# RWKV-7 and S5 trunk on one core: token scale moved behind the FFN's first products, and token norms cut to 64 columns

## Reference, cut to what matters

```
def rmsnorm(x, g):
    y = xf * lax.rsqrt(jnp.mean(xf * xf, axis=-1, keepdims=True) + NORM_EPS)
    return (y * g)
# rwkv7: keys' norm
kk = kk / jnp.maximum(jnp.linalg.norm(kk, axis=-1, keepdims=True), 1e-12)
# layer
h = h + mix
hn = rmsnorm(h, norm_ffn[i])
ffn = (silu(hn @ w_gate) * (hn @ w_up)) @ w_down      # D=1024, F=2816
h = h + ffn
```

## Time and profile before

| | |
|---|---|
| median of three executions | 1642.6 us |
| the profiled execution | 1643.39 us |
| its span, first to last instruction | 1641.5 us |
| TensorE busy, VectorE busy, ScalarE busy | 1576.6 (96%), 1270.2 (77%), 958.2 (58%) us |
| mean granted TensorE clock | 0.979 of full speed |

### The profile page before, as it was taken

The page is one execution under the profiler, slowest core; times in us unless marked ns, Lnnn a source line. Parts: engine busy times, 40 slices in busy tenths (PEclk is TensorE's granted clock), DMA queues, the critical chain, the costliest instruction groups (busy, mean ns, idle before and its releaser), DMA issues.

```text
span 1641.5 us, 28526 instructions
## 1 busy us (share of the span) xinstructions
PE 1576.6 (96%) x12396; PEld 1359.9 (83%) x12396; DVE 1270.2 (77%) x1430; ACT 958.2 (58%) x1054; POOL 87.8 (5%) x71
## 2 busy tenths in 40 slices
PE   8898798899998999999999999999999999999997
PEld 7698787899998788788888888888888888888885
DVE  6675432996865546998988888888888898988985
ACT  2723211666441036776776776776776777777673
POOL 0006101100001600000000000000000000000000
PEclk9999999999996999999999999999999999999999
DMA  7230002444525064799799799799799799799791
GB/s 287 94 130 28 4 3 104 153 182 164 184 90 207 20 265 187 290 384 372 295 392 384 284 392 399 272 389 401 268 392 402 269 390 401 276 384 401 276 382 68
DMA packets 72493, 421.19 MB, mean 257 GB/s; under 512 B 5024, under 2 KB 5152, under 8 KB 37424
## 3 DMA queue, kind: packets, MB, share of 16 engines
q1 hardware_dynamic: 72016, 418.26, 65.5%
q0 software_dynamic: 352, 1.10, 0.2%
HBM read 418.29 MB, written 1.05 MB: 255 GB/s over the span
## 4 chain that ended last, share of the span: by engine, by line
PE 91%; DVE 4%; POOL 2%; issue 1%; ACT 1%; DVEq 0%; POOLq 0%
PE PS L1285 37%; PE PS L1298 18%; PE PS L1100 11%; PE PS L1208 3%; PE PS L1314 2%; PE PS L733 2%; PE PS L1085 2%; PE PS L710 2%; PE PS L1291 1%; PE PS L887 1%; PE PS L754 1%; PE PS L692 1%; PE PS L904 1%; DVE LOA L1791 1%; PE PS L1174 1%
## 5 line engine op out<-in xcount | busy, mean ns | idle before, releaser
L1791 DVE TENSOR_TENSOR LOA<-EXA,WH 128x2048 fp32r<-128x2048 f32 x224 | 504.7, 2289 | 94.1 <-ACT WH L598 94.1
L598 ACT ACTIVATE WH<-EXA 128x2048 fp32r<-128x2048 f32 x224 | 416.9, 1909 | 6.4 <-DMA EXA<-in_wmoe 6.2
L1285 PE MATMUL PS<-WH,XGH 128*128 128x512 f32 x896 | 360.6, 403 | 0.0
L1285 PE MATMUL PS<-WH,XGL 128*128 128x512 f32 x896 | 350.6, 391 | 0.0
L1285 PE MATMUL PS<-LOA,XGH 128*128 128x512 f32 x896 | 350.0, 391 | 0.0
L1797 DVE TENSOR_TENSOR LOB<-EXB,WH 128x1024 fp32r<-128x1024 f32 x224 | 264.3, 1222 | 8.6 <-ACT WH L602 8.5
L602 ACT ACTIVATE WH<-EXB 128x1024 fp32r<-128x1024 f32 x224 | 224.2, 1052 | 0.0
L1285 PEld LDWEIGHTS PS<-WH,XGL 128*128 128x128 f32 x896 | 168.2, 188 | 35.7
L1285 PEld LDWEIGHTS PS<-WH,XGH 128*128 128x128 f32 x896 | 168.4, 188 | 33.4 <-DVE XGL L1889 1.8
L1285 PEld LDWEIGHTS PS<-LOA,XGH 128*128 128x128 f32 x896 | 168.8, 188 | 31.2
L1298 PE MATMUL PS<-WH,MHH 128*128 128x512 f32 x448 | 174.6, 390 | 3.8 <-DVE MHL L1885 3.8
(11 more groups left out here) (413 smaller groups left out, 2410.9 us busy)
## 6 DMA issues: line engine op xcount, KB each, us to landing
EXA<-in_wmoe SPq DMA_DIRECT2D x112, 2048.0 KB, 8.6
EXB<-in_wmoe SPq DMA_DIRECT2D x112, 1024.0 KB, 8.1
FRA<-in_wffn SPq DMA_DIRECT2D x22, 1024.0 KB, 5.9
RING<-in_wsq SPq DMA_DIRECT2D x16, 1024.0 KB, 4.9
FRB<-in_wffn SPq DMA_DIRECT2D x22, 512.0 KB, 3.8
GLUW<-in_wglu SPq DMA_DIRECT2D x8, 1024.0 KB, 12.5
...
```

The source lines that it names most:

```text
L598: act.activation(WH[:, n % 4, 0:NARROW], EXA[PAIR_SLOT[n // 2]][:, n % 2, :], ACT.Copy).then_inc(S("m_ahi"), 1)
L1285: mm = pe.matmul(PS[:, p % 2, :], x[:, k, :], w, start=k == 0 and m == 0, stop=k == KC - 1 and m == 2)
L1791: tt(LOA[slot][:, n % 2, :], EXA[slot][:, n % 2, :], WH[:, n % 4, 0:NARROW].bitcast(F32), ALU.subtract)\
```

## The change

- Norm 1: FH and FL are now taken from `HT * gain` without the token scale, pair by pair while the output projection runs. The scale is multiplied onto both halves of gate and up's sums in one VectorE instruction per block (`FGU`, 128x512, out of PSUM), ahead of Silu, which now reads SBUF and waits for that instruction. VectorE multiplies the halves afterwards. Norm 1's last sums stand between gate and up of block 0. FFN slots are swapped so that block 0's weights can be loaded after item 12 and cut into high and low during items 14.
- Norms 0, 2, 4: the sums go to four strips of 32 partitions with 64 tokens each, NT has 64 columns, and a new `spread_rows` brings four strips back to 128 partitions in four banks, from which the products read.
- `spread` of the keys' norm stands behind split projection 2.
- FFN adds: four instructions, one per bank, each as soon as its bank's last matmul is done; squares in four.
- Item 12: halves in turn within each chunk. Item 13 writes bank 5 instead of 0.

```diff
+        SUM_BANK = (7, 7, 3, 0, 4)
+        SPREAD_BANK = {0: 3, 2: 4, 4: 0}
+        VARIED, SUMMED = (1, 3, 4, 6, 7), (1, 3, 4, 6, 7)
+        QT = T // 4
+        def spread_scale(n, chunks):
+            first = SPREAD_BANK[n]
+            return PS[:, first:first + 4, 0:QT].unsqueeze(1).to_broadcast([P, chunks, 4, QT])
@@ SyncE
                 if t < 2:
-                    sp.wait_ge(S("used"), 15)
+                    sp.wait_ge(S("used"), 13 + t)
...
                 sp.dma_start(FRA[:, t % 2, :], wffn[t][:, 0:NARROW]).then_inc(S(f"fa_in{t % 2}"), 16)
-                if t >= 2:
+                if t < 2:
+                    sp.wait_ge(S("used"), 15)
+                else:
                     sp.wait_ge(S("f_blo"), t - 1)
@@ ScalarE, output projection
             for t in range(4):
                 act.wait_ge(S("h_out"), t + 1)
+                for j in (2 * t, 2 * t + 1):
+                    act.activation(FH[:, j, :], HT[:, j, :], ACT.Copy, scale=prm("ffn0", j)).then_inc(S("f_hi"), 1)
                 square(1, SQB, slice(2 * t, 2 * t + 2))
+                if t == 1:
+                    ffn_hi_a(0, 0)
+                    ffn_hi_a(0, 1)
             act.wait_ge(S("used"), 16)
-            ffn_hi_a(0, 0)
+            ffn_hi_a(1, 0)
             root(1)
-            ffn_hi_a(0, 1)
-            ffn_hi_a(1, 0)
-            for n in range(4):
-                pair = slice(2 * n, 2 * n + 2)
-                act.wait_ge(S("n_out"), 8 + 2 * (n + 1))
-                act.activation(flat(FH[:, pair, :]), flat(HNF[:, pair, :]), ACT.Copy).then_inc(S("f_hi"), 1)
             ffn_hi_a(1, 1)
             ffn_hi_b(0)
@@ ScalarE, FFN
             for t in range(NFFN):
-                act.wait_ge(S("f_ps"), t + 1)
-                act.activation(FSG[:, t % 2, :], half(t % 3, 0), ACT.Silu).then_inc(S("f_silu"), 1)
+                act.wait_ge(S("f_mul"), 2 * t + 1)
+                act.activation(FGU[:, t % 2, 0, :], FGU[:, t % 2, 0, :], ACT.Silu).then_inc(S("f_silu"), 1)
                 round_back(t, 0)
                 if t + 2 < NFFN:
                     ffn_hi_a(t + 2, 0)
-                act.wait_ge(S("f_mul"), t + 1)
-                act.activation(FHH[:, t % 2, :], FHF[:, t % 2, :], ACT.Copy).then_inc(S("f_hh"), 1)
+                act.wait_ge(S("f_mul"), 2 * t + 2)
+                act.activation(FHH[:, t % 2, :], FGU[:, t % 2, 1, :], ACT.Copy).then_inc(S("f_hh"), 1)
...
-            for n, h in enumerate(halves):
-                act.wait_ge(S("h_out"), 5 + n)
-                square(2, SQB, h)
+            for g in range(NG):
+                act.wait_ge(S("h_out"), 5 + g)
+                square(2, SQ2, slice(2 * g, 2 * g + 2))
@@ TensorE
+                        for q in range(4):
+                            mm = pe.matmul(PS[32 * q:32 * q + 32, SUM_BANK[n], 0:QT], one[:, 0:32], sq[:, k, q * QT:(q + 1) * QT],
+                                           start=start and k == 0, stop=stop and k == KC - 1, skip_group_check=True)
...
+            def spread_rows(n):
+                pe.wait_ge(S("n_var"), VARIED[n] + 1)
+                for q in range(4):
+                    rows = slice(32 * q, 32 * q + 32)
+                    row = ROW0[rows, :] if n == 0 else CON[rows, C_SPR:C_SPR + P]
+                    mm = pe.matmul(PS[:, SPREAD_BANK[n] + q, 0:QT], row, NT[rows, 0:QT], start=True, stop=True)
+                mm.then_inc(S("n_sum"), 1)
...
             project_split(1, XRH, XRL)
+            project_split(2, XRH, XRL)
             pe.wait_ge(S("sig"), 16)
             pe.wait_ge(S("kk"), 3)
             for j in BY_QUARTER:
                 mm = spread(j, 4 + j // 2)
             mm.then_inc(S("kk_ps"), 1)
-            project_split(2, XRH, XRL)
             project_split(3, XRH, XRL)
...
+                steps = [(h, k) for k in range(KC) for h in range(2)] if t == 12 else [(h, k) for h in range(2) for k in range(KC)]
...
-            norm_part(1, SQB, 3, False, True, 2)
...
                 for h in range(2):
                     if t == 0 and h == 1:
+                        norm_part(1, SQB, 3, False, True, 2)
                         pe.wait_ge(S("f_alo"), 2)
...
+                    if t == NFFN - 1 and n in (1, 3, 5):
+                        mm.then_inc(S("f_ps"), 1)
...
             ffn_down(NFFN - 1)
-            pe.wait_ge(S("h_out"), 6)
-            norm(2, SQB)
+            for g in range(NG):
+                norm_part(2, SQ2, g, g == 0, g == NG - 1, 2)
+            spread_rows(2)
@@ VectorE
+            def scale_of_tokens(n):
+                dve.wait_ge(S("n_sum"), SUMMED[n])
+                ts(NT[:, 0:QT], PS[:, SUM_BANK[n], 0:QT], 1.0 / D, NORM_EPS, ALU.mult, ALU.add).then_inc(S("n_var"), 1)
                 dve.wait_ge(S("n_std"), n + 1)
+                dve.reciprocal(NT[:, 0:QT], NT[:, 0:QT]).then_inc(S("n_var"), 1)
+                dve.wait_ge(S("n_sum"), SUMMED[n] + 1)
...
             for t in range(4):
                 dve.wait_ge(S("used"), 12 + t + 1)
                 tt(flat(HT[:, 2 * t:2 * t + 2, :]), flat(HT[:, 2 * t:2 * t + 2, :]), PS[:, W_BANK[t], :], ALU.add).then_inc(S("h_out"), 1)
+                if t == 2:
+                    ffn_lo_a(0, 0)
+                    ffn_lo_a(0, 1)
+                dve.wait_ge(S("h_out"), t + 1)
+                for j in (2 * t, 2 * t + 1):
+                    dve.wait_ge(S("f_hi"), j + 1)
+                    stt(FL[:, j, :], HT[:, j, :], prm("ffn0", j), FH[:, j, :].bitcast(F32), ALU.mult, ALU.subtract).then_inc(S("f_lo"), 1)
+            dve.wait_ge(S("n_sum"), SUMMED[1])
+            ts(NT[:, :], half(SUM_BANK[1], 0), 1.0 / D, NORM_EPS, ALU.mult, ALU.add).then_inc(S("n_var"), 1)
             ffn_lo_a(1, 0)
+            dve.wait_ge(S("n_std"), 2)
+            link(dve.reciprocal(NT[:, :], NT[:, :]))
+            by_token = NT[:, :].unsqueeze(1).to_broadcast([P, 2, T])
...
             for t in range(NFFN):
-                dve.wait_ge(S("f_silu"), t + 1)
-                tt(FHF[:, t % 2, :], FSG[:, t % 2, :], half(t % 3, 1), ALU.mult).then_inc(S("f_mul"), 1)
+                dve.wait_ge(S("f_ps"), t + 1)
+                tt(FGU[:, t % 2, :, :], PS[:, t % 3, :].rearrange("p (a t) -> p a t", a=2), by_token, ALU.mult).then_inc(S("f_mul"), 1)
                 if t + 2 < NFFN:
                     ffn_lo_a(t + 2, 0)
+                dve.wait_ge(S("f_silu"), t + 1)
+                tt(FGU[:, t % 2, 1, :], FGU[:, t % 2, 0, :], FGU[:, t % 2, 1, :], ALU.mult).then_inc(S("f_mul"), 1)
                 dve.wait_ge(S("f_hh"), t + 1)
-                tt(FHL[:, t % 2, :], FHF[:, t % 2, :], FHH[:, t % 2, :].bitcast(F32), ALU.subtract).then_inc(S("f_hl"), 1)
+                tt(FHL[:, t % 2, :], FGU[:, t % 2, 1, :], FHH[:, t % 2, :].bitcast(F32), ALU.subtract).then_inc(S("f_hl"), 1)
...
-            dve.wait_ge(S("used"), NSQ + NFFN)
-            for n, h in enumerate(halves):
-                tt(flat(HT[:, h, :]), flat(HT[:, h, :]), flat(PS[:, 4 + 2 * n:6 + 2 * n, :]), ALU.add).then_inc(S("h_out"), 1)
-            dve.wait_ge(S("h_out"), 6)
-            norm(2, "mix1", HN[:, :, :])
+            for g in range(NG):
+                pair = slice(2 * g, 2 * g + 2)
+                if g < NG - 1:
+                    dve.wait_ge(S("f_ps"), NFFN + g + 1)
+                else:
+                    dve.wait_ge(S("used"), NSQ + NFFN)
+                tt(flat(HT[:, pair, :]), flat(HT[:, pair, :]), PS[:, 4 + g, :], ALU.add).then_inc(S("h_out"), 1)
+            dve.wait_ge(S("h_out"), 8)
+            scale_of_tokens(2)
+            for j in range(KC):
+                one = slice(j, j + 1)
+                stt(by_quarter(HN[:, one, :])[:, 0], by_quarter(HT[:, one, :])[:, 0], prm("mix1", j), spread_scale(2, 1)[:, 0], ALU.mult, ALU.mult)\
+                    .then_inc(S("n_out"), 1)
```

More of the change, by code:

```diff
@@ L699, in norm @@
                 norm_part(n, sq, 1, False, True, KC // 2)
+                spread_rows(n)
             pe.sem_inc(S("scat_ps"), 2)
@@ L1078, in _ @@
                 pe.wait_ge(landed, value)
-                for h in range(2):
-                    for k in range(KC):
-                        if t == 12 and h == 0 and k % 2 == 0:
-                            pe.wait_ge(S("yg"), k // 2 + 1)
-                        if t == 13 and h == 0 and k == 0:
-                            pe.wait_ge(S("yg"), NG)
-                        mm = pe.matmul(half(W_BANK[t - 12], h), w[:, h * D + k * P:h * D + (k + 1) * P], T1[:, k, :],
-                                       start=k == 0, stop=k == KC - 1)
+                steps = [(h, k) for k in range(KC) for h in range(2)] if t == 12 else [(h, k) for h in range(2) for k in range(KC)]
+                for h, k in steps:
+                    if t == 12 and h == 0 and k % 2 == 0:
+                        pe.wait_ge(S("yg"), k // 2 + 1)
+                    mm = pe.matmul(half(W_BANK[t - 12], h), w[:, h * D + k * P:h * D + (k + 1) * P], T1[:, k, :],
```

(38 more changed lines are left out.)

81 lines of the change are left out of this document (38 added, 43 removed).

## The result

The changed kernel takes **1662.5 us** in the median of six executions (1661.62 to 1664.81), the kernel before on the same chip 1645.9 (1641.24 to 1648.58, six executions): a ratio of **1.0108**, with a 95% interval of 1.0091 to 1.0125. It is slower by 1.1%, 17.8 us by the ratio. The forecast had the sign, and 1656.4 us; the measured time lies 6 above that, inside the range of 1645 to 1667. Half of the 6 lies in the base: the forecast added 13.8 us to three executions of 1642.6 us, and the median of six is now 1645.9. The change itself costs 16.6 us by the medians and 17.8 by the ratio, where 13.8 were forecast. The profiled execution took 1662.57 us, its span is 1660.7; against the 1643.39 of the profiled execution before that is +19.2, where the working came to +13.8.

A forecast was written before the change was run, and what follows sets the result against it. TensorE was taken as the bound, 91% of the span. -2.8 - 5.5 + 30.9 - 6.0 - 2.8 = +13.8 us on the profiled 1643.4 gave 1657.2, stated as 1656.4 because that execution lay 0.8 above the median; range 1645 to 1667.

The forecast's parts named there:

- The step that decided: FFN: VectorE and ScalarE wait for each other over Silu and the weight copies, 3.26 us more VectorE time per block.
- Rival (a): FFN: TensorE stays the bound, all gains stand, -19.6 us in all, total 1623; chance 8%.
- Rival (b): FFN: the clock falls in each wait, a block costs 0.4 to 0.5 us more, total 1666; chance 10%.
- Norm 0: Kernel start: short strip sums and a 64-column reciprocal let L754 start at 11.9, -2.8 us, bounds -1.5 and -3.2.
- the ring's landing: Kernel start: item 1's arrival at 11.8, which L754 needs, was to set its start, taken as 11.9.
- Keys' norm: Keys' spread: split projection 2 fills TensorE's 5.62 us idle there, -5.5 us, bounds -3.5 and -6.5.
- The expected wait of about one us: Projection 4: TensorE may wait for VectorE's low weights, giving back about one us of the gain at the keys' spread.
- Item 12: Item 12's order and bank: TensorE is busy at half clock in its first part, so 0, bounds 0 and -0.5 us.
- Norm 1: Before the FFN: first product at 296.3 instead of 302.6, -6.3 us, containing -5.5 at block 1's start.
- FFN: First to last product 225.3 us instead of 188.5, +36.8; FFN's end +30.9 us, bounds +24 and +37.
- Tail and norm 2: Behind the FFN: drive 6.4 us earlier, 0.4 back to the clock, -6.0, bounds -4 and -11; FFN's tail +0.4.
- Norm 4: Near the kernel's end: products L1967 start at 1633.1 instead of 1635.91, -2.8 us, bounds -2 and -3.2.

The follow-up runs named there:

- experiment 1: Changed kernel with ScalarE's high copies of gate's and up's weights for block t+2 moved ahead of Silu: 1635.7 us, ratio 0.9929.
- experiment 2: Changed kernel with only the high copy of gate's weights for block t+2 moved ahead of Silu: 1640.2 us in one execution.
- experiment 8: experiment 1 with VectorE's low part of up's weights of block t+2 also moved between the product of the halves and FHL: 1629.9 us, ratio 0.9903.
- experiment 3: Changed kernel with GpSimd's two memsets held back until VectorE is past its small S5 steps: 1660.9 us, ratio 1.0089.
- experiment 7: Kernel before with one edit, the keys' spread moved behind split projection 2: 1639.3 us, ratio 0.9966.
- experiment 4: Changed kernel with norm 1 and the FFN put back as before, all other parts kept: 1628.5 us, ratio 0.9903.
- experiment 5: experiment 4 with norm 1 by strips too (sums in four strips, NT of 64 columns, a spread): 1627.2 us, ratio 0.9882.
- experiment 6: experiment 4 with item 12's halves one after the other again, as in the kernel before: 1627.5 us in one execution.

## Why the prediction was right, and where its terms were off

The step that decided, VectorE and ScalarE handing each other the work, is shown by experiments 1, 2 and 8. Each removes hand-overs and no work, and the periods fall from 11.38 to 9.85, 9.24 and 8.72 in the early blocks, from 10.77 to 9.24 and 8.64 in the late ones. Rival (a), TensorE stays the bound, is refuted for the changed kernel; it describes what the cured order gives. Rival (b), the clock, is not what makes the FFN long. Here are four periods of the changed kernel, blocks 2 to 5, each from one FGU to the next (stretch and length, busy time with its instructions of PE, PEld, DVE, ACT and POOL, granted clock, DMA share, GB/s):

```profile
314.58:325.95 11.37, 8.87 (x74) 8.70 (x73) 8.83 (x13) 6.09 (x9) 0.00 (x0) 1.00 0.42 148
325.95:337.32 11.37, 7.27 (x47) 6.85 (x45) 8.83 (x14) 6.08 (x9) 0.00 (x0) 0.85 0.39 141
337.32:349.17 11.85, 10.09 (x63) 10.12 (x64) 8.83 (x13) 7.04 (x11) 0.00 (x0) 0.71 0.38 133
349.17:361.71 12.54, 11.49 (x145) 11.09 (x144) 9.45 (x15) 7.05 (x11) 0.00 (x0) 1.00 0.41 147
```

The second runs at a lower clock than the first and is as long. The third is 0.48 longer, which is the copy back (L538) between Silu and the weights, and the fourth, the longest, has the full clock: besides a copy back it has two VectorE steps more (L1731 and L1733, 0.7 us from 357.04). So the lower clock costs nothing in these periods. Rival (b) wanted 0.4 to 0.5 in all 21, and the FFN as a whole is 2.0 over the forecast.

The terms ahead of norm 1 and behind norm 2 need care, because executions of the same code differ there. The changed kernel and experiments 1, 2, 3 and 8 have the same instructions up to the last item's add, and the same norm 2 and drive (TensorE's first matmuls of S5). GLUW are the weights of the first 128x256 matmuls behind it. The kernel before and experiment 7 have the old norm 0 and norm 2:

| profiled execution | first product | item 12 starts | to the last item's add | drive to the first GLUW matmul | clock 28 to 30 us behind the drive's start |
|---|---|---|---|---|---|
| before | 14.72 | 252.67 | 31.3 | 42.9 | 0.88 |
| experiment 7 | 13.79 | 245.93 | 32.0 | 42.9 | 0.77 |
| changed kernel | 11.70 | 243.79 | 32.5 | 45.5 | 0.50 |
| experiment 1 | 12.89 | 245.87 | 31.0 | 43.7 | 0.83 |
| experiment 2 | 11.62 | 246.09 | 32.6 | 45.0 | 0.50 |
| experiment 3 | 12.21 | 245.72 | 31.2 | 44.9 | 0.50 |
| experiment 8 | 12.24 | 246.33 | 31.6 | 43.2 | 0.82 |

By the terms, on the profiled execution of the changed kernel:

- **Norm 0**: -3.0, forecast -2.8; -1.8 to -3.1 over the five. Here VectorE's `XK` ended the wait before L781 at 11.70; in experiments 1 (12.89) and 4 (11.70) the ring's landing did, which is the end that the working named. The two lie close together.
- **Keys' norm**: -5.9 (item 12 at 243.79, 8.9 ahead, less norm 0's 3.0), forecast -5.5; alone, in ten executions, -5.6. The 8.9 are the most of the five; the others have 6.3 to 7.0, where the two forecasts together had 8.3. The expected wait of about one us is there: TensorE stands still for 1.37 us before projection 4's first matmul (84.27), which before had no wait; VectorE's low parts idle 1.40 us for ScalarE at 86.70.
- **Item 12**: forecast 0, +1.2 in this execution. From its first matmul to the last item's add 32.5 us instead of 31.3. No engine is waited for; TensorE's granted clock is 0.50 until 248 and 0.61 from 248 to 250, 5.8 us or so, where before it was 0.50 from the start at 252.7 until 256, 3.4 us. The table takes the weight off this number: the same code took 31.0 to 32.6 us, in two of five executions less than the kernel before. A loss by the change isn't shown.
- **Norm 1**: the first product of the FFN comes 12.7 us ahead, 5.0 if item 12's 8.9 and 1.2 are taken out; forecast 6.3. Both are counted against the last item's add, so the spread above doesn't enter. The gap is the step that GpSimd's memset held for 2.42 us. The working took that step's duration from the kernel before, where it stood at 297.91, 3.5 us behind the memsets' end; the change moves it among them. Without it (experiment 3) the first product comes 6.5 us ahead by the same count, and the forecast is met.
- **FFN**: 227.4 us from first to last product, forecast 225.3; before 188.5. Block 0 took 13.31 (13.3), blocks 1 to 8 93.6 (93.7), 11 to 13 33.8 (33.6), 14 to 18 53.9 (53.5), 19 and 20 13.6 (13.6). Blocks 9 and 10 took 19.2 instead of 17.6: there TensorE was the bound, 9.5 a block before too, and I had reckoned VectorE's time only ("TensorE's 8.64 are below all of these" is wrong for these two). That is 1.6 of the 2.0 us. Experiment 3 repeats the periods of blocks 1 to 18 to 0.1 us, so these terms don't have the spread of the others.
- **Tail and norm 2**: forecast -6.0 at the drive's start, of which 0.4 goes back to the clock behind it, -5.6. Measured -5.6 at the drive's start, and behind it 2.6 us go back: the first of the 128x256 matmuls on GLUW starts at 573.44, 23.1 late, against 20.5 at the drive. The drive's 512 matmuls take 27.59 us instead of 26.61, the matmuls on `TAP` behind them 11.93 instead of 10.82. How much goes back differs between executions of the same code: 0.3 to 2.6 us over the five of the table, 1.8 to 2.2 in experiments 4 to 6, which have this norm 2 too. It goes with the time at which the full clock comes back: 0.3 and 0.8 where the matmuls on `TAP` are granted 0.82 and 0.83 between 28 and 30 us behind the drive's start (experiments 8 and 1), 1.8 or more where it is still 0.50 there, as in all others.
- **Norm 4**: -2.7, forecast -2.8.

These make -3.0 - 5.9 + 1.2 - 5.0 + 38.9 - 5.6 + 2.6 - 2.7, +20.5; the experts' stages give 1.2 back between 570 and 1646, which leaves the 19.2 of the profile. Against the forecast's +13.8 that is 5.4 more, and no single step makes it: +2.0 in the FFN, +1.3 in norm 1, +1.2 in item 12, +2.6 at norm 2 and the drive, less 0.5 in norm 0, keys' norm and norm 4 together, and less the 1.2 at the end. The first two are errors of the working, shown above. The other two are as large as the spread of the same code, and the 19.2 of the profiled pair is itself 1.4 more than the 17.8 of all executions.

The working also added its bounds wrongly. It says +4 and +24; the bounds of the terms as they stand add to 0 and +26. From 1642.6 that would have been some 1642 to 1669 instead of 1645 to 1667, and the measured time lies inside either.

"TensorE: Matmul & The Clock Gate" of the Trainium skill (section "Wait — 56ns, not 53.3ns?") puts the least distance of two matmuls at about 25 ns. The changed kernel's sums take 0.65 us for 32, 20 ns each, and the first product came 3.0 us earlier: the trace is under the page's figure here too.

What stays open: why executions of the same code are granted the full clock at different times, in item 12 and at the drive; only that they are is shown. And nothing was run to keep the clock up through the wait behind norm 2.
